# Queries turned by VectorE in 32x32 squares and placed by DMA, keys still turned by TensorE, in a one-core decoder layer

## The chip, the cores and the metric

The kernel runs on one core of one Trainium2 chip. The metric is the device time of one execution in microseconds (us). The engines are called PE (TensorE), DVE (VectorE), ACT (ScalarE), POOL (GpSimd) and SP (the queue that issues most transfers). "hi" and "lo" are the two parts into which each fp32 operand is split before it is multiplied.

## What is computed

One decoder layer on x of 256 rows and 1024 columns, 16 heads of 64, feed-forward width 2816:

```python
h = rmsnorm(x, attn_norm)
qkv = jnp.einsum('bsd,de->bse', h, w_in).reshape(B, S, 3, N_HEADS, HEAD_DIM)
q = rope(qkv[:, :, 0])
k = rope(qkv[:, :, 1])
v = qkv[:, :, 2]
o_moba = moba_attention(q[:, :, :a], k[:, :, :a], v[:, :, :a])     # causal, heads 0 to 7
o_dil = dilated_mixture(q[:, :, a:], k[:, :, a:], v[:, :, a:])     # masked and weighted, heads 8 to 15
mixed = jnp.concatenate([rmsnorm(o_moba), rmsnorm(o_dil)], axis=-1)
x = x + jnp.einsum('bse,ed->bsd', mixed, w_out)
h = rmsnorm(x, ffn_norm)
x = x + jnp.einsum('bsf,fd->bsd', jax.nn.silu(h @ w_gate) * (h @ w_up), w_down)
return rmsnorm(x, final_norm)
```

`rope(t)` is `t * cos + concat(-t2, t1) * sin` over the two halves of a head. With 256 rows both mixers are dense attention with a mask that differs by group of 8 heads.

## The kernel before

**Blocks and pairs.** All weights pass through a ring of 12 slots as blocks of 128 x 512. Two blocks are a pair: SP loads it (512 KB, L497), ACT rounds it to `w_hi` (L954), DVE subtracts to get `w_lo` (L1265), and PE multiplies each block in three products (`w_hi,x_hi`, `w_lo,x_hi`, `w_hi,x_lo`, L638 to L640) for each half of 128 rows, so six matmuls of 512 columns per block. Pair p serves blocks 2p and 2p+1. PE waits for `lo_ready` of the pair at each even block. Blocks 0 to 47 make queries, keys and values of two groups of heads (g = 0, 1) in the order q0, k0, q1, k1, v0, v1, eight blocks each (the first two are interleaved and end with blocks 9 and 15); blocks 48 to 63 are the output projection, then the feed-forward follows.

**The attention items.** Everything else is hung between the blocks by tables written by hand: `PE_PLAN[i]` is what PE does after block i; `DVE_PLAN[i]` and `ACT_PLAN[i]` are what those engines do at step i, before the pair that they split there (at odd i: DVE pair (i+7)/2, ACT pair (i+9)/2). `PLACE` hangs transfers on SP behind the loads of a third of the ring. Each engine does its list strictly in order.

For each group the items are:
- `rope(g, w, s)`: DVE rotates queries (w = 0) or keys (w = 1) of half s out of PSUM in three instructions (L1316, L1318, L1324) into `rot`.
- `scale(s)`: ACT multiplies the queries of group 0 by 1/rms (L1025), since `rstd` comes too late for the table; the tables of the later rotations are multiplied by `rstd` on DVE (L1333).
- `turn(g, w, s)`: PE transposes the four 128 x 128 pieces of a half through an identity (L665); ACT copies the result to `qkT_first` (half 0 only, L1034) and to `qkT_hi` (L1037); DVE makes `qkT_lo` (L1341 or L1344).
- `score(g, u)`: PE multiplies queries and keys (u = 0 in plain fp32, L688; u = 1, 2 in three products, L691 to L693); DVE adds the mask and takes the maximum (L1359); ACT takes the exponential (L1046).
- `squares(g, T)`: DVE transposes the probabilities in 32 x 32 squares (`STREAM_TRANSPOSE`, L1370), and four transfers of 64 KB (`place`, L578 on SP, L1068 on ACT) put the squares in their partitions.
- `values`: PE multiplies (L715); `norm`: DVE divides by the sums (L1385); `o`, `olo`: ACT and DVE split the result into `o_hi` and `o_lo` (L1055, L1398), which the output projection reads. Its block 56 needs for its second half of rows the last of the four `olo` (`ot_lo` at 4).

## Time and profile before

| | us |
|---|---|
| median of 3 runs | 294.4 (293.92 to 294.6) |
| the profiled execution, whole | 294.3 |
| its span in the trace | 292.5 |
| PE busy / DVE busy / ACT busy / POOL busy | 284.4 / 264.0 / 190.0 / 18.9 |
| share of PE in the chain that ended last | 89% |

The profiled execution's own time exceeds its span by 1.8 us; the change is reckoned against 294.3 us. Busy times are of the whole span; the granted clock of PE is full in every slice. In a timeline row the first number is the start from the span's beginning, the second how long the row lasts; instructions of an engine overlap a little, so the distance between two starts is what one costs its engine.

### The profile page before, as it was taken

What the parts mean: (1) busy time and instruction counts of PE and PEld (TensorE: products, weight loads), DVE (VectorE), ACT (ScalarE), POOL (GpSimd) and SP (SyncE); (2) the same over time, 40 slices, a digit from 0 to 9 for tenths busy, and PEclk for the clock granted to TensorE, in tenths of its full rate; (3) what the DMA queues carried; (4) which work ended last, traced back from release to release, by engine and by line L of the source; (5) the groups of instructions that cost most, each with busy time, mean ns of one, the idle gap of its engine ahead of it and who ended that gap; (6) DMA issues with size and microseconds to landing.
All of it is one profiled execution on the core that took longest, in us unless ns stands there. A gap on an engine that the chain in (4) does not pass through costs nothing.

```text
span 292.5 us, 4124 instructions
## 1 busy us (share of the span) xinstructions
PE 284.4 (97%) x1396; PEld 231.8 (79%) x1396; DVE 264.0 (90%) x425; ACT 190.0 (65%) x321; POOL 18.9 (6%) x29
## 2 busy tenths in 40 slices
PE   7999999999999999999999999999999999999992
PEld 3778878888888787888888878888888888888881
DVE  3788999999798999997698999999999999989895
ACT  3887767837696676767657665757484756756524
POOL 0002000000130520200000000000000000000032
PEclk9999999999999999999999999999999999999999
DMA  7999516797869976557846659595849382710003
GB/s 225 401 422 382 196 55 193 239 282 224 254 179 235 332 234 236 188 173 235 273 182 210 261 162 375 154 380 137 337 106 354 83 341 89 289 28 9 2 0 143
DMA packets 29797, 62.87 MB, mean 215 GB/s; under 512 B 3664, under 2 KB 17232, under 8 KB 28368
## 3 DMA queue, kind: packets, MB, share of 16 engines
q1 hardware_dynamic: 27760, 61.04, 61.2%
q10 hardware_dynamic: 2016, 1.57, 1.7%
q8 instruction: 11, 0.18, 0.2%
q14 instruction: 10, 0.08, 0.1%
HBM read 55.72 MB, written 1.11 MB: 194 GB/s over the span
## 4 chain that ended last, share of the span: by engine, by line
PE 89%; DMA 3%; DVE 3%; ACT 1%; POOL 1%; SPq 1%; issue 1%; POOLq 0%; DVEq 0%
PE bank L638 28%; PE bank L640 27%; PE bank L639 27%; DMA room<-in_first 3%; PE bank L715 2%; PE bank L665 1%; DVE xs L1609 1%; PE bank L688 1%; SPq L504 1%; PE bank L648 1%; ACT x_hi L987 1%; PE bank L691 0%; DVE rot L1614 0%; POOL xs L1699 0%; DVE w_lo L1265 0%
## 5 line engine op out<-in xcount | busy, mean ns | idle before, releaser
L638 PE MATMUL bank<-w_hi,x_hi 128*128 128x512 f32 x224 | 88.9, 397 | 1.2 <-DVE w_lo L1294 0.8
L640 PE MATMUL bank<-w_hi,x_lo 128*128 128x512 f32 x224 | 87.3, 390 | 0.0
L639 PE MATMUL bank<-w_lo,x_hi 128*128 128x512 f32 x224 | 87.3, 390 | 0.0
L638 PEld LDWEIGHTS bank<-w_hi,x_hi 128*128 128x128 f32 x224 | 42.0, 188 | 12.0 <-DVE w_lo L1294 1.2
L640 PEld LDWEIGHTS bank<-w_hi,x_lo 128*128 128x128 f32 x224 | 42.0, 188 | 8.9
L639 PEld LDWEIGHTS bank<-w_lo,x_hi 128*128 128x128 f32 x224 | 42.1, 188 | 8.2
L1265 DVE TENSOR_TENSOR w_lo<-raw,w_hi 128x1024 fp32r<-128x1024 f32 x32 | 38.3, 1211 | 1.2 <-ACT w_hi L954 1.1
L954 ACT ACTIVATE w_hi<-raw 128x1024 fp32r<-128x1024 f32 x32 | 32.5, 1049 | 9.9 <-issue 9.6
L1421 DVE TENSOR_TENSOR w_lo<-raw,w_hi 128x1024 fp32r<-128x1024 f32 x30 | 36.1, 1216 | 0.5 <-ACT w_hi L1084 0.2
L1101 ACT ACTIVATE rope_b<-bank,rstd 128x256 f32<-128x256 f32 x22 | 10.4, 471 | 33.8 <-PE bank L640 33.5
L1084 ACT ACTIVATE w_hi<-raw 128x1024 fp32r<-128x1024 f32 x30 | 30.9, 1052 | 0.7 <-DMA raw<-in_weights 0.4
L638 PE MATMUL bank<-o_hi,h_hi 128*128 128x512 f32 x64 | 25.0, 390 | 0.0
L640 PE MATMUL bank<-o_hi,h_lo 128*128 128x512 f32 x64 | 24.9, 389 | 0.0
L639 PE MATMUL bank<-o_lo,h_hi 128*128 128x512 f32 x64 | 24.9, 389 | 0.0
L1484 DVE TENSOR_TENSOR o_lo<-room,o_hi 128x1024 fp32r<-128x1024 f32 x18 | 21.2, 1213 | 1.3 <-ACT o_hi L1130 0.8
L1130 ACT ACTIVATE o_hi<-room 128x1024 fp32r<-128x1024 f32 x18 | 18.2, 1052 | 3.9 <-PE bank L640 3.9
L1491 DVE TENSOR_TENSOR o_lo<-room,o_hi 128x1536 fp32r<-128x1536 f32 x8 | 14.0, 1756 | 3.0 <-ACT o_hi L1140 3.0
L1046 ACT ACTIVATE probs<-probs,neg_max 128x128 f32<-128x128 f32 (+1 forms) x32 | 14.1, 444 | 3.0 <-DVE neg_max L1359 3.0
L638 PE MATMUL bank<-qkT_hi,x_hi 128*128 128x512 f32 x40 | 15.6, 389 | 0.0
L639 PE MATMUL bank<-qkT_lo,x_hi 128*128 128x512 f32 x40 | 15.6, 389 | 0.0
L640 PE MATMUL bank<-qkT_hi,x_lo 128*128 128x512 f32 x40 | 15.6, 389 | 0.0
L1140 ACT ACTIVATE o_hi<-room 128x1536 fp32r<-128x1536 f32 x8 | 11.9, 1488 | 4.9 <-PE bank L640 4.8
(158 smaller groups left out, 480.8 us busy)
## 6 DMA issues: line engine op xcount, KB each, us to landing
raw<-in_weights SPq DMA_DIRECT2D x74, 512.0 KB, 5.7
room<-in_weights SPq DMA_DIRECT2D x9, 1024.0 KB, 7.2
room<-room SPq DMA_DIRECT2D x76, 64.0 KB, 2.2
room<-in_first SPq DMA_DIRECT2D x1, 1024.0 KB, 9.1
xs<-in_x SPq DMA_DIRECT2D x2, 512.0 KB, 9.5
rot<-turned_sums SPq DMA_DIRECT2D x8, 128.0 KB, 4.1
raw<-in_weights SPq DMA_DIRECT2D x1, 1024.0 KB, 7.2
room<-in_first SPq DMA_DIRECT2D x2, 384.0 KB, 5.8
```

Of the source, the lines that this page charges most:

```text
L638: pe.matmul(dst, a_hi, w1, start=first, stop=False)
L639: pe.matmul(dst, a_hi, w2, start=False, stop=False)
L640: return pe.matmul(dst, a_lo, w1, start=False, stop=last)
L954: act.activation(w_hi[:, slot:slot + 2, :], raw[:, 2 * pos:2 * pos + 2, :], ACT.Copy).then_inc(hi_ready, 1)
L1046: ins = act.activation(piece, piece, ACT.Exp, bias=neg_max[:, g, half, head:head + 1], scale=-1.0, accum_out=sums[:, g, half, head:head + 1])
L1084: act.activation(gate_up_at(c, 2 * j, 2)[0], raw[:, 2 * at:2 * at + 2, :], ACT.Copy).then_inc(hi_ready, 1)
L1130: act.activation(down_hi[:, 2 * part:2 * part + 2, :], forms_of(c)[:, at:at + 2, :], ACT.Copy).then_inc(down_hi_ready, 1)
L1140: act.activation(second_forms_at(c)[0][:, 0:len(FORMS_B), :], forms_of(c)[:, FORMS_B[0]:FORMS_B[-1] + 1, :], ACT.Copy).then_inc(down_hi_re ...
L1265: dve.tensor_tensor(w_lo[:, slot:slot + 2, :], raw[:, 2 * pos:2 * pos + 2, :], w_hi[:, slot:slot + 2, :].bitcast(f32), ALU.subtract).then_ ...
L1421: dve.tensor_tensor(lo, raw[:, 2 * at:2 * at + 2, :], hi.bitcast(f32), ALU.subtract).then_inc(lo_ready, 1)
L1484: dve.tensor_tensor(down_lo[:, to, :], forms_of(c)[:, at:at + 2, :], down_hi[:, to, :].bitcast(f32), ALU.subtract).then_inc(down_lo_ready, 1)
L1491: dve.tensor_tensor(lo[:, 0:len(FORMS_B), :], forms_of(c)[:, FORMS_B[0]:FORMS_B[-1] + 1, :], hi[:, 0:len(FORMS_B), :].bitcast(f32), ALU.su ...
```

## The change

For queries only, the transposition moves from PE to DVE and the DMA queues.

- The host lays the columns of the query weights out so that, after a 32 x 32 square transposition and four transfers of whole squares, each head's elements stand in the partitions where PE needs them. The rotation tables of the queries are laid out to match, carry the factor 1/8, and are loaded by a new transfer of 256 KB (`q_angles`), issued before `tab`. They are not multiplied by `rstd`, so `scale` now exists for both groups.
- `qturn(g, s)`: one `STREAM_TRANSPOSE` on DVE of `rot[:, 0, s]` into `vals[:, 0, s]`. `q(n)`: four transfers of 64 KB back into `rot[:, 0, s]`, on SP for n = 0, 1, 3 and on ACT for n = 2.
- `qfirst(g)`: ACT copies half 0 of the queries for `score(g, 0)`; that half has no hi and lo any more. `qhi`, `qlo`: ACT and DVE split half 1.
- PE keeps only the turns of the keys.

```diff
 PE_PLAN = {
-    14: [("turn", 0, 0, 0)],
-    17: [("turn", 0, 0, 1), ("turn", 0, 1, 0)],
-    19: [("score", 0, 0)],
+    17: [("turn", 0, 0)],
+    20: [("score", 0, 0)],
...
-    41: [("values", 0, 0), ("values", 0, 1), ("values", 0, 2)],
-    42: [("score", 1, 1), ("score", 1, 2)],
+    43: [("values", 0, 0), ("values", 0, 1), ("values", 0, 2)],
+    44: [("score", 1, 1), ("score", 1, 2)],
...
 PLACE = {
+    (2, 0): [("q", 0)],
+    (2, 1): [("q", 1)],
     (2, 2): [("place", 0)],
...
-    (3, 2): [("back", 0), ("out", 1)],
+    (3, 2): [("q", 3), ("out", 1), ("back", 0)],
...
+            sp.dma_start(q_angles[:], table[:, C_ROPE_Q:C_ROPE_Q + 2 * SH * P]).then_inc(in_angles, 16)
             sp.dma_start(tab[:, 0:C_MASK], table[:, 0:C_MASK]).then_inc(in_tab, 16)
...
+                elif kind == "q":
+                    sp.wait_ge(q_turned, n + 1)
+                    for i in range(JS):
+                        sp.dma_start(q_placed[n % SH][:, i, :, :], q_squares[n % SH][i * SQ:(i + 1) * SQ, :, :]).then_inc(in_q[n % SH], 16)
...
-                    _, g, qk_i, s = it
-                    n = g * 4 + qk_i * 2 + s
-                    if n == 0:
+                    _, g, s = it
+                    if (g, s) == (0, 0):
                         pe.wait_ge(in_tab, 16)
-                    pe.wait_ge(*((rotated, n + 1) if n > 1 else (q_scaled, s + 1)))
...
+                    pe.wait_ge(rotated, g * 4 + 2 + s + 1)
+                    if g:
+                        pe.wait_ge(*((qk_lo, 3) if s else (max_ready, SC_TILES)))
...
+                elif kind == "qfirst":
+                    g = it[1]
+                    act.wait_ge(in_q[0], 16 * JS * (g + 1))
+                    if g:
+                        act.wait_ge(scored, 1)
+                    act.activation(qT_first.rearrange("p h (i b) -> p h i b", i=JS), q_placed[0], ACT.Copy).then_inc(q_first, 1)
...
+                elif kind == "qhi":
+                    g = it[1]
+                    act.wait_ge(in_q[1], 16 * JS * (g + 1))
...
+                    act.activation(q_hi.rearrange("p h (i b) -> p i h b", i=JS), q_placed[1],
+                                   ACT.Copy).then_inc(qk_hi, 1)
...
+                elif kind == "qturn":
+                    _, g, s = it
+                    dve.wait_ge(q_scaled, g * 2 + s + 1)
+                    if g:
+                        dve.wait_ge(in_q[s], 16 * JS)
+                    dve.transpose(q_squares[s].rearrange("p j (x b) -> p x j b", b=SQ),
+                                  rot[:, 0, s, :].rearrange("p (x j a) -> p x j a", j=JS, a=SQ)).then_inc(q_turned, 1)
+                elif kind == "qlo":
+                    g = it[1]
+                    dve.wait_ge(qk_hi, g * 3 + 2)
+                    hi, lo = (t.rearrange("p h (i b) -> p i h b", i=JS) for t in (q_hi, q_lo))
+                    dve.tensor_tensor(lo, q_placed[1], hi.bitcast(f32), ALU.subtract).then_inc(qk_lo, 1)
```

How this moves instructions shows at three places. First DVE between the rotation of group 0's second half of queries and its first half of keys, before:

```order
L1324 TENSOR_TENSOR rot<-rope_a,rope_b 128x512 [waits rope_mul]
L1265 TENSOR_TENSOR w_lo<-raw,w_hi 128x1024 [waits hi_ready] x2
L1333 TENSOR_SCALAR front<-tab,rstd 128x128 [waits rstd_ready]
L1333 TENSOR_SCALAR front<-tab,rstd 128x128
L1316 TENSOR_TENSOR rope_a<-bank,front 128x512 [waits rotated,rotary_ready,blk_done]
L1318 TENSOR_TENSOR rope_b<-bank,front 128x512
```

and after:

```order
L1360 TENSOR_TENSOR rot<-rope_a,rope_b 128x512 [waits rope_mul]
L1386 STREAM_TRANSPOSE vals<-rot 128x4x4x32 [waits q_scaled]
L1295 TENSOR_TENSOR w_lo<-raw,w_hi 128x1024 [waits hi_ready]
L1386 STREAM_TRANSPOSE vals<-rot 128x4x4x32 [waits q_scaled]
L1295 TENSOR_TENSOR w_lo<-raw,w_hi 128x1024 [waits hi_ready]
L1369 TENSOR_SCALAR front<-tab,rstd 128x128 [waits rstd_ready]
L1369 TENSOR_SCALAR front<-tab,rstd 128x128
L1352 TENSOR_TENSOR rope_a<-bank,front 128x512 [waits rotary_ready,rotated,blk_done]
```

Two transpositions, each behind a wait for ACT's scaling, now stand ahead of pairs 8 and 9 and so of the keys' rotation.

Second DVE in group 1, from the pair that block 32 needs (pair 16, the first `w_lo` row) to the one that block 34 needs, before:

```order
L1370 STREAM_TRANSPOSE room<-probs 128x4x4x32 [waits in_p0,exp_done]
L1265 TENSOR_TENSOR w_lo<-raw,w_hi 128x1024 [waits hi_ready]
L1370 STREAM_TRANSPOSE room<-probs 128x4x4x32 [waits in_p1,exp_done]
L1265 TENSOR_TENSOR w_lo<-raw,w_hi 128x1024 [waits hi_ready]
L1316 TENSOR_TENSOR rope_a<-bank,front 128x512 [waits rotated,blk_done]
```

and after:

```order
L1416 STREAM_TRANSPOSE room<-probs 128x4x4x32 [waits in_p0,exp_done]
L1295 TENSOR_TENSOR w_lo<-raw,w_hi 128x1024 [waits hi_ready]
L1416 STREAM_TRANSPOSE room<-probs 128x4x4x32 [waits in_p1,exp_done]
L1386 STREAM_TRANSPOSE vals<-rot 128x4x4x32 [waits in_q0,q_scaled]
L1386 STREAM_TRANSPOSE vals<-rot 128x4x4x32 [waits in_q1,q_scaled]
L1295 TENSOR_TENSOR w_lo<-raw,w_hi 128x1024 [waits hi_ready]
```

Two transpositions are new ahead of pair 17.

Third PE around `values` of group 0 (L715, now L728), where the rows of blocks are told apart by the wait for `lo_ready` at an even block, here block 42. Before:

```order
L715 MATMUL bank<-room,vals 64x128 [waits v_taken,in_p1,in_p0]
L715 MATMUL bank<-room,vals 64x128 x7
L715 MATMUL bank<-room,vals 64x128 [waits qk_lo,in_p3,in_p2]
L715 MATMUL bank<-room,vals 64x128 [waits in_p5,in_p4]
L638 MATMUL bank<-w_hi,x_hi 128x512 [waits lo_ready]
L691 MATMUL bank<-qkT_hi 128x256 [waits max_ready,qk_lo]
```

and after:

```order
L654 MATMUL bank<-w_hi,x_hi 128x512 [waits lo_ready]
L655 MATMUL bank<-w_lo,x_hi 128x512
L728 MATMUL bank<-room,vals 64x128 [waits v_taken,in_p1,in_p0]
L728 MATMUL bank<-room,vals 64x128 [waits qk_lo,in_p3,in_p2]
L728 MATMUL bank<-room,vals 64x128 [waits in_p5,in_p4]
L704 MATMUL bank<-qkT_hi 128x256 [waits max_ready,qk_lo]
```

Blocks 42 and 43 now come before `values`, block 44 between `values` and `score(1, 1)`; before, `values` stood ahead of block 42 and the scores behind it (of the matmul rows of a block only the first ones are shown).

## Rows read from the trace of the kernel before

**Rows 1.** The page's head and its busy times: us, share of the span, instructions.
```profile
span 292.5 us, 4124 instructions
PE 284.4 (97%) x1396; PEld 231.8 (79%) x1396; DVE 264.0 (90%) x425; ACT 190.0 (65%) x321; POOL 18.9 (6%) x29
```

**Rows 2.** Timeline of PE, 31 to 38 us: start, us, engine, line, operation.
```profile
31.44 1.03 PE L665 MATMUL bank<-tab,rot 128*128 128x128 f32 x8
...
32.54 0.40 PE L639 MATMUL bank<-w_lo,x_hi 128*128 128x512 f32 x1
...
37.73 0.60 PE L665 MATMUL bank<-tab,rot 128*128 128x128 f32 x4
```

**Rows 3.** Windows: us, busy (x) of PE, PEld, DVE, ACT, POOL, clock, DMA share, GB/s.
```profile
13.00:20.00 7.00, 6.64 (x30) 5.18 (x29) 6.22 (x9) 6.74 (x10) 0.00 (x0) 1.00 1.02 416
```

**Rows 4.** Timeline of ACT, 19 to 40 us; in brackets idle time before, and its releaser.
```profile
19.13 1.06 ACT L980 ACTIVATE probs<-xs 128x1024 bf16<-128x1024 f32 x1 [0.22 <-DMA xs<-in_x]
...
24.04 0.72 ACT L1025 ACTIVATE rot<-rot,rstd 128x512 f32<-128x512 f32 x1 [2.51 <-POOL rstd L1666]
24.67 2.94 ACT L954 ACTIVATE w_hi<-raw 128x1024 fp32r<-128x1024 f32 x3
...
38.37 0.60 ACT L1037 ACTIVATE qkT_hi<-bank 128x512 fp32r<-128x512 f32 x1 [2.65 <-PE bank L665]
...
39.81 0.39 ACT L1046 ACTIVATE probs<-probs,neg_max 128x128 f32<-128x128 f32 x1
```

**Rows 5.** Timeline of DVE, 25 to 42 us.
```profile
25.74 2.36 DVE L1265 TENSOR_TENSOR w_lo<-raw,w_hi 128x1024 fp32r<-128x1024 f32 x2 [0.39 <-ACT w_hi L954]
28.02 0.48 DVE L1333 TENSOR_SCALAR front<-tab,rstd 128x128 f32<-128x128 f32 x2
28.91 0.69 DVE L1316 TENSOR_TENSOR rope_a<-bank,front 128x512 f32<-128x512 f32 x1 [0.41 <-PE bank L640]
...
30.24 0.69 DVE L1324 TENSOR_TENSOR rot<-rope_a,rope_b 128x512 f32<-128x512 f32 x1
...
41.48 0.71 DVE L1370 STREAM_TRANSPOSE room<-probs 128x512 f32<-128x512 f32 x1 [0.59 <-ACT probs L1046]
```

**Rows 6.** Timeline of DVE: pair 16, and later squares, keys' lo and pair 21.
```profile
53.73 1.18 DVE L1265 TENSOR_TENSOR w_lo<-raw,w_hi 128x1024 fp32r<-128x1024 f32 x1
...
67.64 0.70 DVE L1370 STREAM_TRANSPOSE room<-probs 128x512 f32<-128x512 f32 x1
68.27 0.65 DVE L1341 TENSOR_TENSOR qkT_lo<-vals,qkT_hi 128x512 fp32r<-128x512 f32 x1
68.84 1.22 DVE L1265 TENSOR_TENSOR w_lo<-raw,w_hi 128x1024 fp32r<-128x1024 f32 x1
```

**Rows 7.** Timeline of PE: starts of blocks 32 and 34, a turn, and values.
```profile
55.91 0.39 PE L638 MATMUL bank<-w_hi,x_hi 128*128 128x512 f32 x1
...
58.63 0.39 PE L638 MATMUL bank<-w_hi,x_hi 128*128 128x512 f32 x1
...
64.50 0.60 PE L665 MATMUL bank<-tab,rot 128*128 128x128 f32 x4
...
71.86 2.84 PE L715 MATMUL bank<-room,vals 128*64 128x128 f32 x48
```

**Rows 8.** Timeline of DVE: score(1, 1), a norm, and the last olo.
```profile
77.25 0.42 DVE L1359 CUSTOM_DVE_ANT_0 probs<-bank,tab 128x256 f32<-128x256 f32 x1 [0.61 <-PE bank L693]
...
91.85 0.69 DVE L1385 TENSOR_TENSOR room<-bank,rot 128x512 f32<-128x512 f32 x1 [0.31 <-PE bank L715]
...
100.31 1.63 DVE L1398 SCALAR_TENSOR_TENSOR o_lo<-room,gain,o_hi 128x128 fp32r<-128x128 f32 x4 [0.22 <-ACT o_hi L1055]
```

**Rows 9.** Timeline of PE: block 56, first matmul of the second half of rows.
```profile
102.07 0.42 PE L638 MATMUL bank<-w_hi,o_hi 128*128 128x512 f32 x1
```

**Rows 10.** Timeline of SP: one set of squares placed; and landing times of L497's loads.
```profile
42.22 2.59 SPq L578 DMA_DIRECT2D room<-room  x4
...
DMA to landing us min/median/max: 3.6/5.7/10.1
```

More of the change, by code:

```diff
@@ L163 @@
 PE_PLAN = {
[L164 to L174 removed]
+    17: [("turn", 0, 0)],
+    20: [("score", 0, 0)],
+    21: [("turn", 0, 1)],
+    25: [("score", 0, 1), ("score", 0, 2)],
+    35: [("turn", 1, 0)],
+    37: [("score", 1, 0)],
+    38: [("turn", 1, 1)],
+    43: [("values", 0, 0), ("values", 0, 1), ("values", 0, 2)],
+    44: [("score", 1, 1), ("score", 1, 2)],
     51: [("osum", 0), ("values", 1, 0)],
@@ L182 @@
     6: [("rope", 0, 0, 0)],
-    9: [("rope", 0, 0, 1)],
+    9: [("rope", 0, 0, 1), ("qturn", 0, 0)],
+    11: [("qturn", 0, 1)],
     12: [("rope", 0, 1, 0)],
-    13: [("turn", 0, 0, 0)],
-    16: [("turn", 0, 0, 1), ("rope", 0, 1, 1)],
-    17: [("turn", 0, 1, 0)],
-    18: [("score", 0, 0)],
-    21: [("squares", 0, 0), ("turn", 0, 1, 1)],
+    16: [("rope", 0, 1, 1)],
+    17: [("turn", 0, 0)],
+    18: [("score", 0, 0), ("qlo", 0)],
+    21: [("squares", 0, 0), ("turn", 0, 1)],
     23: [("squares", 0, 1), ("rsum", 0, 0), ("score", 0, 1)],
@@ L192 @@
     25: [("rope", 1, 0, 0), ("squares", 0, 2), ("rope", 1, 0, 1), ("squares", 0, 3)],
-    27: [("squares", 0, 4)],
+    27: [("squares", 0, 4), ("qturn", 1, 0), ("qturn", 1, 1)],
     28: [("rope", 1, 1, 0)],
-    29: [("turn", 1, 0, 0)],
-    30: [("turn", 1, 0, 1)],
     31: [("rsum", 0, 1), ("rope", 1, 1, 1)],
     32: [("squares", 0, 5), ("score", 1, 0)],
-    34: [("squares", 1, 0), ("turn", 1, 1, 0)],
-    37: [("squares", 1, 1), ("turn", 1, 1, 1)],
+    35: [("qlo", 1)],
+    34: [("squares", 1, 0), ("turn", 1, 0)],
+    37: [("squares", 1, 1), ("turn", 1, 1)],
     38: [("rsum", 1, 0)],
@@ L221 @@
 ACT_PLAN = {
-    3: [("scale", 0)],
-    13: [("scale", 1)],
-    14: [("turn", 0, 0, 0)],
-    16: [("turn", 0, 0, 1)],
-    18: [("turn", 0, 1, 0)],
-    20: [("turn", 0, 1, 1)],
+    3: [("scale", 0, 0)],
+    9: [("scale", 0, 1)],
+    18: [("qfirst", 0), ("turn", 0, 0)],
+    19: [("qhi", 0)],
+    20: [("turn", 0, 1)],
     22: [("score", 0, 0), ("score", 0, 1)],
     23: [("score", 0, 2)],
-    31: [("turn", 1, 0, 0)],
-    33: [("turn", 1, 0, 1)],
-    34: [("turn", 1, 1, 0)],
-    35: [("place", 4)],
-    36: [("turn", 1, 1, 1), ("score", 1, 0)],
+    25: [("scale", 1, 0)],
+    27: [("scale", 1, 1)],
+    32: [("q", 2)],
+    34: [("turn", 1, 0)],
+    35: [("qfirst", 1), ("place", 4), ("qhi", 1)],
+    36: [("turn", 1, 1), ("score", 1, 0)],
     37: [("take", 0)],
@@ L296, in build @@
         qkT_hi = sb("qkT_hi", [P, 2, HPAIRS, SEQ], f32r)
+        with nc.sbuf_tensor("q_angles", [P, 2 * SH * P], f32) as q_angles:
+            pass
         qkT_lo = sb("qkT_lo", [P, 2, HPAIRS, SEQ], f32r)
-        qkT_first = vals[:, 1, :, :].rearrange("p a (h s) -> p a h s", h=HPAIRS)
+        q_hi, q_lo = (t[:].rearrange("p a h s -> p (a h s)")[:, NB:2 * NB].rearrange("p (h s) -> p h s", h=HPAIRS)
+                      for t in (qkT_hi, qkT_lo))
+        kT_first = vals[:, 1, 1, :].rearrange("p (h s) -> p h s", h=HPAIRS)
+        qT_first = vals[:, 1, 0, :].rearrange("p (h s) -> p h s", h=HPAIRS)
+        q_placed = [rot[:, 0, s, :].rearrange("p (i h b) -> p i h b", i=JS, h=HPAIRS) for s in range(SH)]
+        q_squares = [vals[:, 0, s, :].rearrange("p (j c) -> p j c", j=JS) for s in range(SH)]
         probs = sb("probs", [P, 4, NB])
@@ L427, in build @@
         p_turned = sem("p_turned")
+        q_turned = sem("q_turned")
+        q_first = sem("q_first")
+        in_q = [sem(f"in_q{s}") for s in range(SH)]
         in_p = [sem(f"in_p{i}") for i in range(LANDINGS)]
         turned = sem("turned")
-        qk_first = sem("qk_first")
+        k_first = sem("k_first")
         qk_lo = sem("qk_lo")
@@ L1728 @@
         table[:, s0:s0 + half] = -np.sin(a)
+        for n, (first, second) in enumerate(((np.cos(a), np.cos(a)), (-np.sin(a), np.sin(a)))):
+            both = np.concatenate([first, second], axis=1).reshape(P, 16, 1, JS) * np.float32(HEAD_DIM ** -0.5)
+            q0 = C_ROPE_Q + (2 * s + n) * P
+            table[:, q0:q0 + P] = np.broadcast_to(both, (P, 16, 2, JS)).transpose(0, 3, 2, 1).reshape(P, P)
     t, k = np.arange(SEQ)[:, None], np.arange(SEQ)[None, :]
@@ L1745, in quads, with queries @@
         return [np.concatenate(list(w[i:i + QUAD]), axis=1) for i in range(0, len(w), QUAD)]
+    def queries(block):
+        return block.reshape(P, HPAIRS, 2, 16, JS).transpose(0, 1, 4, 2, 3).reshape(P, NB)
     loads = []
@@ L1751 @@
         c0 = w * D_MODEL + g * GW
-        qkv.append(get["w_in"][k * P:(k + 1) * P, c0:c0 + NB])
+        block = get["w_in"][k * P:(k + 1) * P, c0:c0 + NB]
+        qkv.append(block if w else queries(block))
     loads += quads(qkv)
```

120 lines of the change are left out of this document (62 added, 58 removed).

## The prediction

> **What bounds the kernel now.** First the page's busy times [rows 1]: PE is busy for 284.4 of 292.5 us, DVE for 264.0. So nearly all that PE no longer does could be won, but DVE has little room for more. That average hides where the room is, so I then read the timelines of PE, DVE and ACT side by side from 13 to 110 us, where all the edits lie, and asked at each even block by how much the pair it needs was early. The reader is to see that PE never stops there, but that DVE is late enough at a few places for small shifts to stop it:
> - Pair 16 is subtracted at 53.73 + 1.18 = 54.91 [rows 6]; block 32, which needs it, starts at 55.91 [rows 7]. Room: 1.0 us.
> - Pair 21 ends at 68.84 + 1.22 = 70.06 [rows 6]; block 42 comes after `values`, which start at 71.86 and last 2.8 us [rows 7]. Room: 4.6 us, of which `values` are most.
> - The last `olo` ends at 100.31 + 1.63 = 101.94 [rows 8]; block 56's second half starts at 102.07 [rows 9]. Room: 0.1 us. From `score(1, 1)` on DVE at 77.25 to this `olo` there are 24.7 us, and in them DVE stood idle for PE only once, for 0.31 us [rows 8].
>
> The last is the place that decides: PE goes on at 102 us when DVE has done a fixed list that starts with `score(1, 1)`, and `score(1, 1)` is where PE's plan puts it.
>
> **Unit costs.** Eight transposes on PE: the third product after them starts 32.54 - 31.44 = 1.10 us later, less one matmul of 0.23, so 0.87 for eight and 0.44 for four [rows 2]. A block: between the turn at 64.50 and `values` at 71.86 lie a turn and five blocks, so (7.36 - 0.44 - 0.1)/5 = 1.36 us [rows 7]. A pair on DVE: two start at 25.74 and the next instruction at 28.02, so 1.14 each, and 1.22 until the last is done [rows 5, 6]. `STREAM_TRANSPOSE` of 128 x 512: 68.27 - 67.64 = 0.63; a lo: 68.84 - 68.27 = 0.57 [rows 6]. New `rope` layout: same elements, taken as equal. From one engine's end to another's start 0.05.
>
> **What the change removes and adds.** PE loses 4 turns of queries: -1.74 us, all of it on the path as long as PE doesn't wait. DVE loses two lo (-1.1) and gains four transposes (+2.5): +1.4 us. ACT: per group a first copy, a hi and, in group 1, two scalings and four DMA issues are new and three copies go; it is busy for 65% of the time [rows 1], so I look only at what it makes late. Four sets of four transfers are added, and 256 KB of tables.
>
> **Step 1, the keys' turn waits: 0.9 us.** The tables go ahead of x in a queue that is full (DMA share 1.02, 416 GB/s) [rows 3]: 256 KB / 416 GB/s = 0.63 us. ACT already waits for x, and then for `rstd` until 24.04 [rows 4]; both shift, so the first scaling runs from 24.67 to 25.39, pair 8's hi behind it until 26.35, the second scaling, behind that, until 26.97. DVE: first `qturn` 25.4, pair 8 at 26.4, second `qturn` 27.5, pair 9 at 28.2, until 29.3; rescaled tables 0.52, so the keys' rotation starts at 29.82 instead of 28.91, where PE was what it waited for, and ends 30.24 + 0.69 - 28.91 = 2.02 later [rows 5], at 31.84. PE has block 17 done at 31.44 - 0.44 = 31.00 [rows 2] and now needs just these keys. It starts the turn at 31.90: 0.90 lost. If the tables cost no time on the queue, 0.4.
>
> **Step 2, block 32 waits: 1.3 us.** From turn to turn PE took 37.73 - 31.44 = 6.29 us [rows 2]. The plan now has four transposes less between them and a block more: 6.29 - 0.44 + 1.36 = 7.2, so `turn(0, 1)` is at 39.12, 1.39 later than 37.73. ACT waits for it (2.65 us idle, for PE), then for nothing until the exponentials at 39.81 [rows 4], and DVE's `squares(0, 0)` waits for those until 41.48 (idle 0.59) [rows 5]. So this comes at 42.87; DVE's own list would be there at 29.82 + 2 rotations of 1.93 + 4 pairs of 1.14 + two lo and the score, 2.9 = 41.1. From there to pair 16 DVE has no idle time and the list has the same length, so the pair is done at 54.91 + 1.39 = 56.30. PE covers the stretch to block 32 in 55.91 - 37.73 = 18.18 us, less two turns and a block: 15.95, arrival at 55.07. It waits until 56.36: 1.3 lost.
>
> **Step 3, block 34: 0.2 us.** Behind pair 16 DVE has a squares, two new transposes and pair 17: 55.12 + 1.10 + 3 x 0.63 + 1.22 = 59.33; PE arrives at 56.36 + 2.83 = 59.19.
>
> **Step 4, block 42: 1.3 us.** Block 34 to the turn in front of the exponentials was 64.50 - 58.63 = 5.87 [rows 7]; two blocks more are in between now: 59.39 + 5.87 + 2.73 = 67.99. From turn to `squares` it takes 0.64 (37.73 to 38.37), 0.5 for the copy, and 41.48 - 39.81 = 1.67 [rows 2, 4, 5]: 70.8. DVE is through with pair 20 at about 69.4 (from 59.25: two rotations, pairs 18 to 20, squares, sums, score) and waits; then squares, two lo and pair 21: 70.8 + 0.63 + 1.17 + 1.22 = 73.8. PE is at block 42 after a turn and three blocks, 72.6, since `values` no longer stand ahead of it. It waits until 73.9: 1.3 lost. Before, the same lateness would have been hidden under `values`. The DMA issues on ACT (a set takes SP 2.6 us [rows 10]) end before the turn's result is there, so I cost them at nothing; that cover is some 0.5 us.
>
> Sum so far: 0.9 + 1.3 + 0.2 + 1.3 - 1.74 = +2.0 us.
>
> **Step 5, from +2.0 to +4.5 us.** `values` start after blocks 42 and 43: 73.9 + 2.83 = 76.7. `score(1, 1)` on DVE came 77.25 - 71.86 = 5.39 after the start of `values` [rows 7, 8] and still has one block between: 82.1, which is 4.8 later than 77.25. DVE's list of 24.7 us follows; it can absorb the 0.31 in which it waited for PE, and PE had 0.1 to spare. So block 56's second half starts 4.5 us later than 102.07. PE loses that piecewise (at the first and second `olo`, blocks 48, and here), which is why the sum over PE's own waits up to block 44 is not the end of it. Behind it everything hangs on PE and is unchanged.
>
> **Time: 294.3 + 4.5 = 298.8 us** (the profiled execution lies 0.1 below the median).
>
> Per piece of 128 x 128 these rows give 0.87/8 = 0.11 us on PE and 0.63/4 = 0.16 on DVE [rows 2, 6]. The Trainium skill ("VectorE: DVE Perf Modes", The three transpose paths) has it the other way round for bf16, 390 ns on TensorE and 311 ns on VectorE, in blocks of 32 only. As an estimate by its figures 16 pieces would free 6.2 us of PE for 5.0 of DVE, and the sum would be some 4.5 us lower, 294.3; the rows are of these operations in fp32, so they decide. The same page's rules for kernel authors say to transpose 128 x 128 on TensorE if PSUM will do as destination, which speaks against the change.
>
> **Bounds.** Below: none of steps 1 to 4 costs anything (x in time, exponentials in time). PE is at block 42 at 71.86 - 1.74 = 70.1, `values` at 73.0, `score(1, 1)` at 78.3, 1.1 later than before, so +0.7: **295.0**. A gain would need DVE's list behind `score(1, 1)` to shrink too, and no part of it is touched. Above: the transfers of `q(0)`. I took 2 to 3 us to land; weights took up to 10.1 [rows 10] while the queue was full. Issued from 26.1, in 2.5 us, the last at 28.0 and landing 9.4 later at 37.4, they hold ACT's `qfirst` and the keys' copy behind it until 38.5, and `score(0, 0)`, due at 31.90 + 0.44 + 3 x 1.36 = 36.4, comes 2.1 later: 301.
>
> **Rivals.**
> - *The saving is paid in full* (other side): PE 97%, DVE 90% [rows 1], PE's chain loses 1.74: 292.6. Its place is `olo` against block 56: it holds if the last `olo` is done by 100.3. Point of decision: `score(1, 1)` must reach DVE by 75.7; by the plan it is at 78.3 at best. For: PE is busy throughout. Against: 0.1 us of room. Chance 0.07. The Trainium skill ("Perfetto Trace Analysis", Identifying the Most-Contended Engine) says that matmul busy time misleads and weight-load busy time is to be read; that is 79% here, below DVE's 90%, so by it DVE is the contended engine and gets 1.4 us more: an estimate of 295.7.
> - *Gain and loss cancel*, within 0.2% (0.6 us, about what a measurement of this kernel can tell from no change): 294.3. Chance 0.04.
> - *Only the order costs*: steps 1 to 4 are mostly absorbed, 295.0 to 297.0. For: each is a difference of two long sums. Chance 0.17.
> - *Forecast*: 297.0 to 300.2, chance 0.62.
> - *Transfers late*: 301 or so. For: the queue's backlog. Against: by 30 us the backlog has gone, and the q transfers are small. Chance 0.10.
>
> The range 295.0 to 300.2 leaves out 0.07 + 0.04 + 0.10. Faster 0.07, same 0.04, slower 0.89.
>
> **What would show it.** In the new profile: PE's `turn(0, 0)` idle before it, some 0.9 us, released by DVE's `rot`; PE idle at blocks 32 and 42 for over 1 us each, released by `w_lo`; DVE idle over 1 us before `squares(0, 0)` and `squares(1, 0)`, for ACT; `score(1, 1)` on DVE near 82; block 48 and block 56's second half behind `o_lo`. Wrong if PE has no idle time at 32 and 42, or `score(1, 1)` starts before 79, or ACT's `qfirst` waits over 1 us for a DMA.

## The result and the profile after

| | before | after |
|---|---|---|
| median | 294.37 us (293.6 to 294.6, 5 runs) | 299.84 us (299.17 to 300.57, 5 runs) |
| ratio to before | | 1.0202, 95% interval 1.0184 to 1.0220 |
| profiled execution, its span | 294.3, 292.5 | 300.44, 298.6 |

The change costs 5.5 us by the medians. The forecast was 298.8 us in a range of 295.0 to 300.2. The median is 1.0 us above the forecast; the ratio, applied to the 294.3 us from which the forecast was reckoned, gives 300.2 us, at the upper end of the range. The profiled execution was slower than the median by 0.6 us, so its timelines show somewhat more loss than the typical execution has. The page's head, busy times and the shares of the chain that ended last, of after:

```profile
span 298.6 us, 4112 instructions
...
PE 285.1 (95%) x1380; PEld 230.1 (77%) x1380; DVE 265.0 (89%) x427; ACT 190.1 (64%) x321; POOL 18.4 (6%) x29
...
PE 68%; DVE 12%; DMA 7%; ACT 4%; issue 3%; POOL 2%; ACTq 1%; SPq 1%; POOLq 0%; DVEq 0%
```

DVE's busy time rose by 1.0 us, PE's by 0.7 although four turns are gone [rows 1]; neither is the story. The story is the chain: PE's share fell from 89% to 68%, and DVE, DMA, ACT and issue took its place. PE now waits, and this is for whom (the waits of PE: us in total, times, longest):

```profile
PE bank L654 <- DVE w_lo L1295: 3.3, 4, 1.3
PE bank L805 <- DVE warm L1289: 1.2, 1, 1.2
PE bank L654 <- DVE o_lo L1444: 1.1, 1, 1.1
PE bank L654 <- issue: 0.8, 1, 0.8
PE bank L701 <- issue: 0.5, 1, 0.5
PE bank L678 <- DVE rot L1360: 0.3, 1, 0.3
PE bank L654 <- DVE xs L1455: 0.3, 1, 0.3
```

The wait for `warm` is in both kernels. ("issue" means that the trace shows nothing that PE waited for. For the 0.8 us, at 87.97, it was the first `olo`: that one ended at 86.73 + 1.13 = 87.86 on DVE.) Timeline of PE after, at the places that the prediction named (start, us, engine, line, operation, idle time before and its releaser):

```profile
31.13 0.63 PE L678 MATMUL bank<-tab,rot 128*128 128x128 f32 x4 [0.34 <-DVE rot L1360]
...
38.39 0.60 PE L678 MATMUL bank<-tab,rot 128*128 128x128 f32 x4
...
55.64 0.50 PE L654 MATMUL bank<-w_hi,x_hi 128*128 128x512 f32 x1 [1.17 <-DVE w_lo L1295]
55.98 0.39 PE L655 MATMUL bank<-w_lo,x_hi 128*128 128x512 f32 x1
...
65.30 1.16 PE L701 MATMUL bank<-vals 64*128 64x128 f32 x16 [0.52 <-issue]
...
73.90 0.50 PE L654 MATMUL bank<-w_hi,x_hi 128*128 128x512 f32 x1 [1.31 <-DVE w_lo L1295]
...
76.85 0.88 PE L728 MATMUL bank<-room,vals 128*64 128x128 f32 x12
...
87.97 0.47 PE L654 MATMUL bank<-w_hi,o_hi 128*128 128x512 f32 x1 [0.76 <-issue]
...
90.12 0.50 PE L654 MATMUL bank<-w_hi,o_hi 128*128 128x512 f32 x1 [0.52 <-DVE w_lo L1295]
...
108.03 0.50 PE L654 MATMUL bank<-w_hi,o_hi 128*128 128x512 f32 x1 [1.14 <-DVE o_lo L1444]
```

These answer to [rows 2, 7 and 9]. Block 32 is at 55.64 with 1.17 us idle, block 42 at 73.90 with 1.31, and block 56's second half at 108.03, 5.96 later than 102.07. From there to the end of the span it is 190.6 us, before 190.4: everything was lost by 108 us. Timeline of DVE after, which answers to [rows 5, 6 and 8]:

```profile
30.29 0.69 DVE L1360 TENSOR_TENSOR rot<-rope_a,rope_b 128x512 f32<-128x512 f32 x1
...
42.14 0.71 DVE L1416 STREAM_TRANSPOSE room<-probs 128x512 f32<-128x512 f32 x1 [1.49 <-ACT probs L1076]
...
70.83 0.71 DVE L1416 STREAM_TRANSPOSE room<-probs 128x512 f32<-128x512 f32 x1 [1.41 <-ACT probs L1076]
...
72.63 1.22 DVE L1295 TENSOR_TENSOR w_lo<-raw,w_hi 128x1024 fp32r<-128x1024 f32 x1
...
82.24 0.42 DVE L1405 CUSTOM_DVE_ANT_0 probs<-bank,tab 128x256 f32<-128x256 f32 x1 [0.60 <-PE bank L706]
...
99.13 1.23 DVE L1295 TENSOR_TENSOR w_lo<-raw,w_hi 128x1024 fp32r<-128x1024 f32 x1 [2.17 <-ACT w_hi L967]
...
106.36 1.61 DVE L1444 SCALAR_TENSOR_TENSOR o_lo<-room,gain,o_hi 128x128 fp32r<-128x128 f32 x4 [0.22 <-ACT o_hi L1085]
```

`score(1, 1)` is at 82.24 and the last `olo` done at 107.97. Between them lie 25.73 us, 1.04 more than the 24.69 of before [rows 8], and the new item among them is 2.17 us of idle time for a `w_hi` (pair 29). ACT's timeline around it, and in front of the two copies of group 1's queries, after:

```profile
19.41 1.06 ACT L993 ACTIVATE probs<-xs 128x1024 bf16<-128x1024 f32 x1 [0.18 <-DMA xs<-in_x]
...
23.98 0.72 ACT L1038 ACTIVATE rot<-rot,rstd 128x512 f32<-128x512 f32 x1 [2.17 <-POOL rstd L1712]
...
64.57 0.63 ACT L1055 ACTIVATE vals<-rot 128x512 f32<-128x512 f32 x1 [1.26 <-DMA rot<-vals]
...
67.20 0.63 ACT L1066 ACTIVATE qkT_hi<-rot 128x512 fp32r<-128x512 f32 x1 [1.99 <-PE bank L701]
...
94.15 3.79 ACTq L1098 DMA_DIRECT2D room<-room  x4
98.04 2.01 ACT L967 ACTIVATE w_hi<-raw 128x1024 fp32r<-128x1024 f32 x2 [3.91 <-issue]
```

The hi of pair 29 waits at 98.04 for nothing but ACT's own four DMA issues of the last squares (`place 11`). They take 3.79 us. SP is issuing a set at the same time:

```profile
93.79 3.40 SPq L590 DMA_DIRECT2D room<-room  x4
```

Before, ACT issued the same four in 2.56 us:

```profile
89.33 2.56 ACTq L1068 DMA_DIRECT2D room<-room  x4
```

SP was issuing then too (a set from 88.42 for 2.50 us), so it isn't issuing on two queues at once that made the difference. The length of the list goes with the time that these four issues take: in the nine versions that leave `place 11` at its step, they take 2.54 to 3.79 us and the way from `score(1, 1)` to the end of the last `olo` takes 24.66 to 25.73, and the second less the first is 21.9 to 22.1 us in all nine. In the other four traces of versions of the changed kernel that leave it there the list is 24.70 (issues 2.77), 24.98 (2.88), 25.43 (3.54) and 25.46 (3.57). So the 25.73 of this execution is at the long end.

### The profile page after: what moved, and what is told of

Its sections match the earlier page's. It is cut to its first block, busy times and chain, and to the rows that moved or that the text cites. A ratio compares the mean times of both kernels' runs of the same rounds, so it can differ in the third digit from the quotient of the medians.

```text
span 298.6 us, 4112 instructions
## 1 busy us (share of the span) xinstructions
PE 285.1 (95%) x1380; PEld 230.1 (77%) x1380; DVE 265.0 (89%) x427; ACT 190.1 (64%) x321; POOL 18.4 (6%) x29
## 3 DMA queue, kind: packets, MB, share of 16 engines
q1 hardware_dynamic: 29632, 62.09, 61.3%
HBM read 55.98 MB, written 1.11 MB: 191 GB/s over the span
## 4 chain that ended last, share of the span: by engine, by line
PE 68%; DVE 12%; DMA 7%; ACT 4%; issue 3%; POOL 2%; ACTq 1%; SPq 1%; POOLq 0%; DVEq 0%
PE bank L654 22%; PE bank L655 21%; PE bank L656 21%; DMA xs<-in_x 3%; DVE w_lo L1295 2%; ACT w_hi L967 2%; DMA rot<-vals 2%; PE bank L728 2%; DMA room<-in_first 2%; DVE probs L1405 1%; DVE room L1416 1%; ACT probs L1076 1%; DVE xs L1655 1%; DVE o_lo L1444 1%; DVE rot L1360 1%
## 5 line engine op out<-in xcount | busy, mean ns | idle before, releaser
L654 PE MATMUL bank<-w_hi,o_hi 128*128 128x512 f32 x32 | 13.3, 415 | 2.7 <-DVE o_lo L1444 1.1
```

Source lines behind the costliest of these rows:

```text
L654: pe.matmul(dst, a_hi, w1, start=first, stop=False)
```

## The experiments

The theory (A) after the result: PE's wins by the removed turns are given back where a pair or an `olo` from DVE comes late; DVE is late because ACT hands over late; and that is set by the order in which PE's plan delivers, and by DMA issues in ACT's queue. The rivals: the change's own costs, that is VectorE's added work, the queries' transfers, or the tables. In two profiled executions of one kernel block 8 can start up to 1.1 us apart (16.42 to 17.54 over these runs; 17.23 before, 16.90 after), so times of different traces are compared from block 8's start.

**1. The new order alone**, in the kernel before:

```diff
-    41: [("values", 0, 0), ("values", 0, 1), ("values", 0, 2)],
-    42: [("score", 1, 1), ("score", 1, 2)],
+    43: [("values", 0, 0), ("values", 0, 1), ("values", 0, 2)],
+    44: [("score", 1, 1), ("score", 1, 2)],
```

> The kernel before with one part of the change alone: values of group 0 after block 43 instead of 41, and the scores (1, 1) and (1, 2) after block 44 instead of 42. Nothing else moves; all queries are still turned by TensorE. Theory A (PE's order decides, through VectorE's fixed list from score(1, 1) to the last olo): score(1, 1) comes 2 blocks = 2.7 us later, 0.4 us of it is absorbed, so about 296.7 us, and block 56's second half waits over 1 us for o_lo. Theory B (the order is innocent, the loss comes from the added work on VectorE, ACT and the queues): 294.4 us, within 0.4.

Measured: 296.79 us beside 293.8, ratio 1.0111 [1.0092, 1.0129]: 3.0 us more by the medians, 3.3 by the ratio. With not one query turned by DVE, the timelines of DVE and PE show waits at the same places as after, though shorter ones for pair 29 and the last `olo`:

```profile
79.68 0.42 DVE L1359 CUSTOM_DVE_ANT_0 probs<-bank,tab 128x256 f32<-128x256 f32 x1 [0.60 <-PE bank L693]
...
95.51 1.22 DVE L1265 TENSOR_TENSOR w_lo<-raw,w_hi 128x1024 fp32r<-128x1024 f32 x1 [0.92 <-ACT w_hi L954]
```
```profile
104.40 0.50 PE L638 MATMUL bank<-w_hi,o_hi 128*128 128x512 f32 x1 [0.62 <-DVE o_lo L1398]
```

`score(1, 1)` comes 2.4 us later than at 77.25, and block 56's second half 2.3 later than at 102.07 (counted from block 8 it is 2.7 and 2.6). This is step 5's rule shown by itself: what moves `score(1, 1)` moves the end.

**2. The old order of values and scores, in the kernel after.**

```diff
-    43: [("values", 0, 0), ("values", 0, 1), ("values", 0, 2)],
-    44: [("score", 1, 1), ("score", 1, 2)],
+    41: [("values", 0, 0), ("values", 0, 1), ("values", 0, 2)],
+    42: [("score", 1, 1), ("score", 1, 2)],
```

> The changed kernel with values back after block 41 and the scores (1, 1) and (1, 2) after block 42. Theory A: block 42's wait for pair 21 (1.3 us) falls under values, but values (0, 1) now wait about as long for the keys' last lo; score(1, 1) reaches VectorE near 79.6 instead of 82.2, so about 2.6 us less than the changed kernel, 297.2. Theory B: no gain, 299.8.

Measured: 297.71 us beside 293.8, ratio 1.0136 [1.0121, 1.0151]: 0.66% or 1.9 us less than after (2.1 by the medians). `score(1, 1)` is at 79.75 on DVE. It is less than experiment 1's 3.0 to 3.3 us. Part of the reason is that PE, now at `values` earlier, waits there 1.0 us for ACT's copy of the values (`v_taken`) and 0.5 us for a keys' lo.

**3. Group 0's scores one block earlier, in the kernel after.**

```diff
-    20: [("score", 0, 0)],
-    21: [("turn", 0, 1)],
-    25: [("score", 0, 1), ("score", 0, 2)],
+    19: [("score", 0, 0)],
+    20: [("turn", 0, 1)],
+    24: [("score", 0, 1), ("score", 0, 2)],
```

> The changed kernel with score(0, 0), turn(0, 1) and the scores (0, 1) and (0, 2) back after blocks 19, 20 and 24 (now 20, 21 and 25). Theory A: the exponentials start 1.4 us earlier, VectorE's 1.5 us idle time before squares(0, 0) goes, block 32 waits at most 0.2 us instead of 1.2, and all that follows is earlier: about 298.6 us. Theory B (ACT is late because it waits for the placed queries, 2.35 us): no gain, 299.8.

Measured: 298.51 us, ratio 1.0164 [1.0137, 1.0192]. Block 32's wait is gone, as step 2 says it must if `turn(0, 1)` causes it. The time falls by 0.4% or 1.1 us, but the interval overlaps a little with that of after (1.0184 to 1.0220), so the gain itself isn't clear of noise. PE's wait at `score(1, 0)` for the late queries rises from 0.5 to 1.2 us: 0.7 us of what is won at 32 is lost again at the next late hand-off. Counted from block 8, `score(1, 1)` is only 0.6 us earlier than after (64.75 for 65.34); the rest of the gain in this trace is a list of 24.70 us instead of 25.73, with DVE idle 1.15 us for pair 29 instead of 2.17.

**4. Both turns of queries done twice, group 0 and 1, in the kernel before** (1.74 us of work added on PE).

```diff
-                    for p in range(HPAIRS):
+                    for p in [*range(HPAIRS)] * (1 if qk_i else 2):
```

> The kernel before with each of the four query turns done twice on PE, into the same places: 16 transposes more. Theory A: they are worth 0.44 us per four as the timeline says and nothing hides them: 294.4 + 1.74 = 296.1 us. Rival (PE's time there is partly hidden behind something else, so removing the turns could not have paid 1.74): under 295.3.

Measured: 296.06 us beside 293.8, ratio 1.0085 [1.0064, 1.0106], +2.3 us by the medians for 1.74 us of transposes. So a transpose added to PE is paid in full and somewhat over. That is one side only: it doesn't show that one taken away is won, and in experiment 11 it wasn't.

**5. The tables behind x, in the kernel after.**

```diff
-            sp.dma_start(tab[:, 0:C_MASK], table[:, 0:C_MASK]).then_inc(in_tab, 16)
...
                 sp.dma_start(xs[:, s, :], x[0, s * P:(s + 1) * P, :]).then_inc(in_x[s], 16)
+            sp.dma_start(tab[:, 0:C_MASK], table[:, 0:C_MASK]).then_inc(in_tab, 16)
```

> The changed kernel with the transfer of tab (256 KB) issued behind x, so that with the new query tables the queue ahead of x is as full as before. Theory A (the new tables delay x by 0.6 us, hence rstd, the first scaling, both first transposes on VectorE, and the keys' rotation): ACT's first sum of squares starts 0.6 us earlier measured from block 8, PE's 0.34 us before turn(0, 0) goes, 0.4 us less: 299.4. Theory B (VectorE's own work ahead of the keys' rotation makes the wait): unchanged, 299.8.

Measured: 299.64 us beside 294.18, ratio 1.0173 [1.0152, 1.0194], which overlaps with the 1.0202 of after: no more than some tenths. Timeline of PE:

```profile
16.42 0.50 PE L654 MATMUL bank<-w_hi,x_hi 128*128 128x512 f32 x1 [0.28 <-DVE w_lo L1295]
...
30.52 0.63 PE L678 MATMUL bank<-tab,rot 128*128 128x128 f32 x4 [0.18 <-DVE rot L1360]
```

From block 8 the turn is at 14.10 us, after 14.23: 0.13 us won. It isn't passed on in this trace, since PE waits 1.28 us for the queries at `score(1, 0)` instead of 0.52.

**6. ACT issues the last squares behind two more pairs, in the kernel after.**

```diff
-    48: [("place", 11)],
+    50: [("place", 11)],
```

> The changed kernel with the last four transfers of squares that ACT issues (3.8 us of ACT there, 2.6 before) moved from step 48 to step 50, so behind pair 29's hi. Theory A (VectorE's list from score(1, 1) to the last olo got 1.0 us longer because ACT's issue holds pair 29, for which VectorE idles 2.17 us): that idle time goes, up to 1.5 us less at the last olo unless the values wait for these squares, so 298.3 to 299.0. Theory B (the list is set by VectorE's own work): unchanged, 299.8.

Measured: 299.1 us beside 294.18, ratio 1.0163 [1.0144, 1.0181]: by the ratios 0.4% or 1.1 us less than after, with intervals that just don't meet. DVE's 2.17 us of idle time is gone. In DVE's timeline, where `score(1, 1)` is at 82.00, the last `olo` is now done at 105.52:

```profile
82.00 0.42 DVE L1405 CUSTOM_DVE_ANT_0 probs<-bank,tab 128x256 f32<-128x256 f32 x1 [0.61 <-PE bank L706]
103.89 1.63 DVE L1444 SCALAR_TENSOR_TENSOR o_lo<-room,gain,o_hi 128x128 fp32r<-128x128 f32 x4 [0.21 <-ACT o_hi L1085]
```

The list lasts 23.5 us instead of 25.7, which is 2.2 us in this profiled execution (the quickest of this version, 298.24 us) for 1.1 us by the ratios. The two agree better when the 23.5 us are set against the 24.7 and 25.0 us of experiments 3 and 5. So this one line of ACT's table, which the diff doesn't touch, is what carried the list beyond the 24.4 us of the prediction. Here ACT took 2.61 us for the four issues with SP issuing beside it, where after it took 3.79.

**7. Edits 2, 3 and 5 together.**

> The changed kernel with three things set back together: values after block 41 and the scores behind block 42, the first scores and turn(0, 1) one block earlier, and tab behind x. Theory A: the gains of the single ones add, 2.1 + 1.2 + 0.4 = 3.7 us less than the changed kernel, 296.1; it stays above the kernel before because VectorE still has 1.4 us more to do and the queries of group 1 come late. Theory B (one wait takes the place of the other): no better than the best single one, 297.7.

Measured: 296.71 us, ratio 1.0083 [1.0068, 1.0098], 3.1 us less than after by the medians and 3.5 by the ratios. That is near the sum of the three that theory A expected (3.7), so the gains add up almost in full. What is left shows in PE's waits, which move on: 1.0 us for `v_taken`, 0.6 for the queries, 0.5 for `o_lo`, 0.5 for the keys' lo.

**8. VectorE's new work alone, in the kernel before.** Four `STREAM_TRANSPOSE` of the queries into a spare buffer stand at the steps at which the change has them; their result isn't used.

```diff
-    9: [("rope", 0, 0, 1)],
+    9: [("rope", 0, 0, 1), ("spare", 0, 0)],
+    11: [("spare", 0, 1)],
...
-    27: [("squares", 0, 4)],
+    27: [("squares", 0, 4), ("spare", 1, 0), ("spare", 1, 1)],
...
-    13: [("scale", 1)],
+    9: [("scale", 1)],
```

> The kernel before plus the four new transposes on VectorE, at the steps where the change has them, into a place that nothing reads (and the second scaling at ACT's step 9, as in the change). No transfers, no tables, PE unchanged. Theory A (VectorE has little room, so its added work alone costs): 2.5 us more work, of which the room at blocks 34 to 40 (1.3 to 2 us) hides the larger part; 294.6 to 295.4. Theory B (PE is the bound and VectorE's 10% of idle time takes it): 293.8 to 294.2, no change.

Measured: 294.19 us beside 294.18, ratio 1.0009 [0.9998, 1.0019]. Theory A fails: 2.5 us more on an engine that is 90% busy cost nothing that the measurement can tell (0.6 us at most, by the interval), though they stand ahead of pairs 8, 9 and 17. DVE's idle time from 17 to 102 us, summed over the brackets of its timeline, falls from 5.5 us to 3.8: most of the new work lies where DVE had stood waiting, and `score(1, 1)` comes at 77.63, before at 77.25.

**9 and 10. Two sets of DMA issues moved away from ACT's hand-offs**, once in the version of experiment 7 (the first diff) and once in the kernel before (the second):

```diff
-    35: [("qfirst", 1), ("place", 4), ("qhi", 1)],
+    35: [("qfirst", 1), ("qhi", 1)],
...
-    48: [("place", 11)],
+    50: [("place", 11)],
...
-    (3, 2): [("q", 3), ("out", 1), ("back", 0)],
+    (3, 2): [("q", 3), ("place", 4), ("out", 1), ("back", 0)],
```
```diff
-    35: [("place", 4)],
...
-    48: [("place", 11)],
+    50: [("place", 11)],
...
-    (3, 2): [("back", 0), ("out", 1)],
+    (3, 2): [("place", 4), ("back", 0), ("out", 1)],
```

> This is the version with values, scores and tables moved forward (296.7 us), and with two sets of ACT's DMA issues moved besides: the place of squares 4 from ACT to SP, right behind the issues of the queries' second half, and place 11 behind the hi of pair 29. Theory A (what is left of the loss is ACT's hand-offs held by its own DMA issues): the split of the queries' second half, which starts 2.0 us after its predecessor because the issues of place 4 stand between, comes 1.4 us or more earlier; the exponentials of score(1, 0) start before 67.2 instead of 68.44, PE's wait of 1.0 us in front of values goes, DVE's wait of 1.3 us for the hi of pair 29 goes, and the time is 295.0 to 295.6 us. Rival B (what is left is the late landing of the queries, 5 us after their last issue, which neither edit touches): over 296.2 us.

> The kernel before, with the same two edits (place 4 on SP ahead of the sums, place 11 behind the hi of pair 29). It tells whether the two edits help the change alone or any version. Theory A (they pay only where a hand-off from ACT is late, and before there was 1 us of room at block 32 and 4.6 at block 42): within 0.3 us of the kernel before, 293.7 to 294.4. Rival B (DVE's idle time of 0.55 us in front of pair 29 was on the path before too, and so was the set on ACT ahead of the exponentials): 293.0 to 293.5.

Measured: 295.62 us for the change, ratio 1.0038 [1.0025, 1.0051], 1.1 us less than experiment 7 by the medians, 1.3 by the ratios; 294.09 us for the kernel before, ratio 0.9989 [0.9978, 1.0000]. So the two edits pay in the change and hardly elsewhere. But not by the way I expected: counted from block 8 the exponentials of `score(1, 0)` start at 50.8 us, in experiment 7 at 50.9. ACT, rid of the issues, waits 1.65 us for the keys' turn instead, and PE's wait for `v_taken` stays at 0.9 us. So what was gained is `place 11`'s, as in experiment 6: `score(1, 1)` is only 0.1 us earlier from block 8 (61.3 for 61.5), and the list behind it is 24.5 us instead of 25.4, with DVE's 1.29 us of idle time for pair 29 gone.

**11. The second turn of group 1's keys one block earlier**, directly behind `score(1, 0)`, in the version of experiment 9:

```diff
-    37: [("score", 1, 0)],
-    38: [("turn", 1, 1)],
+    37: [("score", 1, 0), ("turn", 1, 1)],
```

> As the version with the issues moved, and the second turn of group 1's keys directly behind score(1, 0), one block (1.36 us) earlier on PE. Theory A (ACT's exponentials of score(1, 0) wait for the copy of that turn): with the copy earlier they start up to 0.6 us earlier, and the time is 0.2 to 0.6 us below the version with the issues moved. Rival B (they wait for the scores' maximum from DVE, which the turn does not move): the same time within 0.2 us.

Measured: 294.38 us beside 294.21, ratio 1.0008 [0.9992, 1.0024]: 1.2 us less than experiment 9 by the medians, 0.9 by the ratios, for one transposition moved by 1.36 us. That is more than the 0.2 to 0.6 us that I expected, by the way that theory A has it: from block 8 the exponentials start at 49.5 us instead of 50.8, and `score(1, 1)` comes at 60.1 instead of 61.3. The whole loss of the change is gone. PE's waits from `turn(1, 0)` to block 56 are down to the one for the queries. Busy times from 17 to 102 us (us, then PE, PEld, DVE, ACT, POOL busy and instructions, clock, DMA share, GB/s), of the kernel before, of after, and of this version:

```profile
17.00:102.00 85.00, 84.77 (x512) 69.62 (x513) 79.20 (x170) 60.29 (x134) 9.67 (x11) 1.00 0.76 244
```
```profile
17.00:102.00 85.00, 80.38 (x479) 64.14 (x479) 74.41 (x160) 57.13 (x127) 6.71 (x7) 1.00 0.75 233
```
```profile
17.00:102.00 85.00, 83.86 (x497) 67.82 (x497) 80.04 (x171) 60.61 (x134) 9.52 (x11) 1.00 0.81 255
```

In the third PE has 0.9 us less to do in the stretch than in the first, and DVE 0.8 us more. Both are at block 56's second half at the same time (101.96 and 102.07; from block 8, 84.96 and 84.84 us). What PE saves, 1.74 us, turns into its stops. By the distances between starts (why these and not the idle time is told at the end) they are 0.9 us at the queries, 0.4 at the keys' `rot`, 0.15 at block 34 and 0.35 within `values` of group 0, which take 3.12 us to the next block instead of 2.77.

**12. Can the change be made to win?** Two edits on experiment 11: the second turn ahead of `score(1, 0)`, and the issues of `place 6` from ACT to SP.

```diff
-    37: [("score", 1, 0), ("turn", 1, 1)],
+    37: [("turn", 1, 1), ("score", 1, 0)],
...
-    38: [("place", 6)],
...
-    (4, 1): [("place", 7), ("out", 2)],
+    (4, 1): [("place", 6), ("place", 7), ("out", 2)],
```

> As the version with the early turn (294.4 us), with two edits more. Place 6 goes from ACT, where its four issues took 4.3 us while SP issued place 5, to SP behind place 5. And PE does the second turn of group 1's keys ahead of score(1, 0), into the time in which it waits for the late queries (0.8 us). Theory A (the hand-offs from ACT are what is left): DVE's waits of 0.72 us for the exponentials and of 0.34 us for a hi behind score(1, 1) go, PE's wait at score(1, 0) falls to 0.4 us, the list from score(1, 1) to the last olo is 23.9 us instead of 24.8, and the time is 293.3 to 293.8 us, below the kernel before (294.2). Rival B (DVE's list itself is what bounds this stretch, in any order of ACT): 294.1 to 294.5.

Measured: 294.62 us beside 294.11, ratio 1.0016 [1.0004, 1.0028]. The time is rival B's, or a little over it. In experiment 11 ACT and SP had issued a set each at the same time; this is ACT's row, and behind it DVE waited 0.72 us for the exponentials:

```profile
72.55 4.26 ACTq L1097 DMA_DIRECT2D room<-room  x4
```

That wait is gone in 12. Of the three rows below, the first has a new wait for a transfer that SP now issues later, and the third one for PE that experiment 11 doesn't have (before: 0.31). The second, at `score(1, 1)`, is in every version (0.61 before).

```profile
75.58 0.69 DVE L1429 TENSOR_TENSOR room<-bank,rot 128x512 f32<-128x512 f32 x1 [0.52 <-DMA rot<-turned_sums]
...
77.83 0.42 DVE L1403 CUSTOM_DVE_ANT_0 probs<-bank,tab 128x256 f32<-128x256 f32 x1 [0.44 <-PE bank L704]
...
92.44 0.69 DVE L1429 TENSOR_TENSOR room<-bank,rot 128x512 f32<-128x512 f32 x1 [0.55 <-PE bank L726]
```

From block 8, `score(1, 1)` comes at 60.3 us, in experiment 11 at 60.1, before at 60.0, and the list from there to the last `olo` takes 24.5, 24.8 and 24.7 us. The time is the rival's, but its reason isn't shown: DVE's list doesn't bound the stretch here. Timelines of DVE and PE in 12:

```profile
100.68 1.63 DVE L1442 SCALAR_TENSOR_TENSOR o_lo<-room,gain,o_hi 128x128 fp32r<-128x128 f32 x4 [0.21 <-ACT o_hi L1083]
```
```profile
102.67 0.39 PE L652 MATMUL bank<-w_hi,o_hi 128*128 128x512 f32 x1
```

The last `olo` is done at 102.31, and block 56's second half starts at 102.67 without having waited. DVE stood idle for 1.0 us within its list besides (0.33, 0.55 and 0.15), and in experiment 6, where nothing held it, the list took 23.5 us. PE doesn't stop from `score(1, 1)` on, so there its own work is the bound. What it lost came before: by 85.18 us from block 8 instead of 84.84, with 1.74 us less to do, 2.1 us went into stops up to `values` of group 0. Whether those can be removed, and the change then wins, was not tried. No version of the change that was run is faster than the kernel before. Not run: the transfers of the queries alone in the kernel before, and another division of DVE's list.

## Why the prediction was right and where it was wrong

The sign and most of the mechanism held: PE stops where the prediction had it stop, and the end is set by DVE's list behind `score(1, 1)`. What failed is a size, that of step 5: the list was taken as fixed at 24.4 us and measured 25.8. A smaller part is PE's wait for the queries at `score(1, 0)`, which was put at nothing and measured 0.6 us. That the old order would have hidden block 42's wait is true of that wait (experiment 2), but only 1.9 of the 5.5 us came back with it. By its steps:

- **Step 1, 0.9 us predicted, 0.46 measured.** The turn came 14.23 us after block 8, and would have come at 31.00 - 17.23 = 13.77 with the first turn taken out. x came late as costed: ACT has it 2.51 us after block 8 instead of 1.90, so 0.61 for 0.63 predicted. But the first scaling, which waits for `rstd`, was only 0.27 us later (7.08 instead of 6.81), not 0.63. I had carried the delay on undiminished to `rstd`; there was slack in between. Experiment 5 has the rest of it: the order of the tables is worth 0.13 us at the turn.
- **Step 2, 1.3 us.** From `turn(0, 1)` to block 32 it took 55.64 - 38.39 = 17.25 us against 15.95 without a wait: 1.30. Experiment 3 removes its cause and the wait with it.
- **Step 3, 0.2 us.** From block 32 to `turn(1, 0)` 61.41 - 55.64 = 5.77 us for four blocks (5.44): 0.33. Of this 0.11 is the restart behind block 32, told below, so 0.2. The list of waits has no line for it.
- **Step 4, 1.3 us.** `squares(1, 0)` at 70.83 (70.8 predicted), pair 21 done at 73.85 (73.8), block 42 at 73.90 (73.9), 1.31 us idle. That the times fit so well is partly luck: PE was 0.33 us early at block 8 and 0.44 better in step 1, and lost 0.5 us and a restart that I had costed at nothing, at `score(1, 0)`, which waited for the queries. One of the three signs by which the prediction was to be called wrong, ACT's `qfirst` waiting over 1 us for a transfer, did appear in group 1 (1.26 us). I had the landing at 2 to 3 us; the four transfers of ACT took 3.6 (median), those of SP 4.1. It shows as PE's 0.5 us at `score(1, 0)`, and as 1.2 to 1.3 us in experiments 3 and 5. ACT's issues, also costed at nothing, did hold a copy (1.99 us idle before 67.20), but as experiment 9 shows nothing hung on it.
- **Step 5 is the term that was mis-sized.** `score(1, 1)` was at 82.24 for 82.1 predicted; counted from block 8 it is 65.34 for 64.87, so 0.5 us late, about the wait for the queries. For the way from there to block 56's second half I took 24.82 us less the 0.31 and 0.1 that could be absorbed, 24.4; it took 108.03 - 82.24 = 25.8 (24.7 and 25.0 in the traces of experiments 3 and 5). I had read DVE's list as a fixed length, since DVE was idle for PE only once in it. But it was idle for ACT too (0.55 us for the hi of pair 29), and ACT's place in it isn't fixed: the four issues of `place 11` took 3.79 us instead of 2.56, and pair 29 came 2.17 us late. Experiment 6 takes this out and gets 1.1 us back. With those 1.1 the forecast would have been 299.9, beside a median of 299.84; that it fits so closely is luck, since the half microsecond for the queries is missing from it.
- **The unit costs** held; the work added on VectorE was rightly not charged as such (experiment 8), except for the 0.2 us at block 34.

The rival *the saving is paid in full* fell on the point given for it: 75.7 for `score(1, 1)`, which came at 82.2. With it falls its estimate from the Trainium skill ("Perfetto Trace Analysis", Identifying the Most-Contended Engine), which charges DVE's occupancy for its 1.4 us more: the runs don't agree, since experiment 8 adds 2.5 us to DVE for a ratio of 1.0009 [0.9998, 1.0019]. *Only the order costs* comes nearest to the truth in its name, not in its size: order, tables and issues together are all of the 5.5 us (experiment 11). The lower bound of 295.0 us was reckoned by PE reaching `score(1, 1)` 1.1 us late with nothing waiting; with the order changed (experiment 11) it reaches it at 77.11 and the time is 294.4, so there is no gain even there. The prediction's reason for that bound, that a gain would need DVE's list to shrink and no part of it is touched, doesn't hold as it stands: moving `place 11` shortens the list (experiment 6), and the last `olo` is then 0.36 us early (experiment 12).
